# A first stage in groups of 4, 4, 4, 2 and 2 row tiles, and a sequence stage with its weight slabs in pairs between the products

## The chip, the cores and the metric

One core of one Trainium2 chip runs the whole layer as one program. The time is the device time of a launch in microseconds (us). The core has a tensor engine (PE), a vector engine (DVE), an activation engine (ACT), GpSimd (POOL) and a sync engine (SP) that issues most DMAs; 16 DMA engines move the data.

## The reference

The reference is one layer of a generative backbone: 256 latent tokens `x` and 256 context tokens `ctx`, 2048 wide, float32. What matters here:

- `adaln`: `silu(c) @ ada_w + ada_b` gives six rows of 2048 (shift, scale and gate for two halves of the layer). For the context only the first two (shift and scale) are needed, with `c_ctx`. `ada_w` is 2048 x 12288, 100 MB.
- `hx = modulate(rmsnorm(x), sh1, sc1)`, and the same for the context. The input projection `hx @ w_in` follows; its columns from `COL_XBC` on feed the state-space branch (a short convolution, then SiLU), 64 columns feed its step sizes `dt`.
- `ssd_chunked`: a state-space scan in chunks of 128 tokens, 32 heads in 4 groups, forward and backward. Per group: the product of the `C` and `B` rows (`cb`), the states of the chunks, decay matrices `exp(cumulative sums)` per head, the product of `cb * decay` with the inputs inside a chunk (diagonal part) and of `C` with the carried state.
- then a gated norm, a second branch (Hyena, long convolutions whose filters come from a small sine network), output projections and a mixture of experts. The change doesn't touch these.

## The kernel before

Weights stream through a ring of 8 slots (`k.raw`, `RAW = 8`), each slot one slab of 128 partitions x 1024 float32, 512 KB. SP issues the loads in a fixed order, and before a load it waits until the old content of that slot was used; so one late user stops all later loads. A weight for a projection is split into a high and a low half (`w_hi` by ACT, `w_lo` by DVE, each a ring of 4) and multiplied three times (`mm3`): high with high, high with low, low with high. The slabs of `ada_w` are used as they are: PE multiplies them with 32 columns (`cpad`) into strips of 32 partitions of one bank, four strips side by side.

First stage (the block that follows line 325). It needs shift and scale for 16 row tiles of 128 rows. The kernel works in 8 groups of 2 row tiles. A group's ring order is 1 projection slab (two row tiles of `w_in`, 512 columns) and 8 modulation slabs (each 4 row tiles of `ada_w` by 256 columns: four for the shift, four for the scale). PE does for a group `ada(g)` (the 8 slabs, bank 4 or 6 in turn), DVE copies the bank to `mrow` (`mod_rows`, line 526), PE turns the rows into columns (`columns`, line 399), DVE adds bias and gain (`mod_columns`, lines 573 and 576). Then ACT writes the high half of the modulated tokens (line 503), DVE the full value and the low half (lines 585 and 592), and `project` (lines 193 to 195, with the `dt` products at 425 and 426) adds this group's part to four banks. PE's order is `ada(g)`, `columns(g - 1)`, `project(g - 2)`. Ahead of it stand `ada(0)`, `ada(1)` and the transposes of the normed tokens (`tokens`, line 408). Between, DVE reduces the argument of the filter network's sine twice (`sine_argument`, lines 530 to 540); `columns(0)` and `columns(3)` wait for it, since it reads the bank that they write. SP issues the first 8 slabs, then 13 small loads of vector rows, then the rest of the slabs.

Sequence stage (the block that follows line 967). A loop of 4 passes, one for each group of 8 heads. Each pass also consumes 32 slabs of `ada_w` (row tile `j // 2`, half `j % 2` of 2048 columns, so rows of 4 KB) into bank 0 for one of the four other modulation rows. PE's order in a pass is: `cb` (line 1006), 8 slabs, the states (lines 1014 to 1017, banks 1 to 4), 8 slabs, the carried products (line 1023, banks 5, 6, 7, 1), the decay blocks `between(0)` and `between(1)` (lines 1034 and 1035, banks 2 and 3), 4 slabs, `within(0)` (line 1044, banks 4 and 5), `between(2)`, 4 slabs, `within(1)`, `between(3)`, 4 slabs, `within(2)`, 4 slabs, `within(3)`. ACT takes the exponential of a decay block (line 1084), DVE mixes it with `cb` (`mixing`, line 1162) for `within`. DVE computes `hin` from the states (lines 1144 to 1151) before the carried products can start, and reads these (lines 1176 to 1182) between `mixing(1)` and `mixing(2)`. `cb` of the next pass waits for ACT's copies of `B` and `C` (lines 1066 and 1067), which wait until DVE has finished `y` of this one (line 1188). At the end of a pass ACT copies bank 0 out (line 1097), POOL adds the bias and stores the row; the block ends only when the last store has landed.

```python
for n in range(RAW, PER_GROUP * GROUPS1 + RAW):
    g, r = (n - RAW) // PER_GROUP, (n - RAW) % PER_GROUP
    if r == 0:
        sp.wait_ge(st.lo_ready, g + 1)
    else:
        sp.wait_ge(s.raw_used, 8 * g + r)
```

## Time and profile before

| | us |
|---|---|
| median of 3 runs | 2368.26 (2367.81 to 2368.78) |
| the profiled execution | 2367.48 |
| its span on the core | 2365.9 |

| engine | busy us | share of the span |
|---|---|---|
| PE | 2195.0 | 93% |
| DVE | 1529.5 | 65% |
| ACT | 1042.3 | 44% |
| POOL | 105.3 | 4% |

The mean granted clock of PE over the span is 0.968 of full speed. The page gives busy shares by slice and the costliest groups; the timeline gives the instructions of one engine in order of time (start in us, duration of the merged entry, engine, line, operation, output from input, number of records, and in brackets the idle time before it and what ended it). A float32 product of PE appears as two records. The view by stretch gives one line for each stretch: the stretch and its length, then for PE, PE's weight loads, DVE, ACT and POOL the busy us and (in brackets) the instructions, then the granted clock (1.00 is 2.4 GHz), the busy share of the DMA engines (it can come out a little over 1) and GB/s.

### The profile page before, as it was taken

Reading aid. Unit: us, or ns where it says so; the run is one execution under the profiler, and the core shown is the slowest. Engines: PE = TensorE matmul, PEld = TensorE weight load, DVE = VectorE, ACT = ScalarE, POOL = GpSimd, SP = SyncE. Lnnn points to the kernel's source line nnn. Section 1 sums busy time; section 2 is a strip of 40 time slices with the busy share of each in tenths; the row PEclk is TensorE's granted clock in tenths of the full one; section 3 lists DMA queues with packets and bytes.
Section 4 is the critical chain, followed back from the end, with each engine's and each line's share of the span. In section 5 each row is a group of like instructions: output and inputs, shape, how many; then the busy total and the mean of one; then the engine's idle time right before and its main releaser. Section 6 shows DMA issues by size and latency. Waiting matters only on the chain. (4 is left out here: it accounts for less than half of the span.)

```text
span 2365.9 us, 32045 instructions
## 1 busy us (share of the span) xinstructions
PE 2195.0 (93%) x12178; PEld 1770.5 (75%) x12178; DVE 1529.5 (65%) x2085; ACT 1042.3 (44%) x1347; POOL 105.3 (4%) x120
## 2 busy tenths in 40 slices
PE   4899998998899999999999999996899999999995
PEld 1568886444689977777778999985688888778784
DVE  2346565566464577877775454554677777899897
ACT  3324332121464433333333334443655555677774
POOL 1000000000000012120201100000000000000000
PEclk9889999999999999999999999997999999999997
DMA  9872324989657654443433565752388888899993
GB/s 308 268 245 91 98 82 150 342 325 355 193 179 232 181 143 137 124 145 116 129 112 107 150 186 167 234 178 92 118 271 265 293 277 264 310 360 386 352 361 135
DMA packets 322075, 500.64 MB, mean 212 GB/s; under 512 B 16710, under 2 KB 185249, under 8 KB 320535
## 3 DMA queue, kind: packets, MB, share of 16 engines
q1 hardware_dynamic: 317158, 481.02, 61.8%
q0 software_dynamic: 4784, 17.83, 2.2%
q8 instruction: 86, 1.41, 0.3%
q14 instruction: 47, 0.38, 0.0%
HBM read 496.65 MB, written 2.13 MB: 211 GB/s over the span
## 5 line engine op out<-in xcount | busy, mean ns | idle before, releaser
L187 DVE TENSOR_TENSOR w_lo<-raw,w_hi 128x1024 fp32r<-128x1024 f32 x712 | 865.5, 1237 | 474.9 <-ACT w_hi L183 457.2
L183 ACT ACTIVATE w_hi<-raw 128x1024 fp32r<-128x1024 f32 x712 | 743.0, 1058 | 684.9 <-PE bank L195 512.2
L193 PE MATMUL bank<-h,w_hi 128*128 128x256 f32 (+1 forms) x896 | 297.8, 332 | 6.9 <-DVE w_lo L187 4.3
L194 PE MATMUL bank<-h,w_hi 128*128 128x256 f32 (+1 forms) x896 | 293.3, 327 | 0.0
L195 PE MATMUL bank<-h,w_lo 128*128 128x256 f32 (+1 forms) x896 | 293.1, 327 | 0.0
L1419 PE MATMUL bank<-h,w_hi 128*128 128x512 f32 x768 | 275.1, 402 | 0.0
L1421 PE MATMUL bank<-h,w_lo 128*128 128x256 f32 x768 | 215.6, 281 | 0.0
L193 PEld LDWEIGHTS bank<-h,w_hi 128*128 128x128 f32 x896 | 174.9, 195 | 21.6 <-DVE w_lo L187 4.5
L194 PEld LDWEIGHTS bank<-h,w_hi 128*128 128x128 f32 x896 | 175.0, 195 | 13.3 <-issue 0.5
L195 PEld LDWEIGHTS bank<-h,w_lo 128*128 128x128 f32 x896 | 174.4, 195 | 13.8
L1419 PEld LDWEIGHTS bank<-h,w_hi 128*128 128x128 f32 x768 | 144.9, 189 | 37.7 <-issue 3.7
L1421 PEld LDWEIGHTS bank<-h,w_lo 128*128 128x128 f32 x768 | 145.6, 190 | 1.4 <-issue 1.4
L193 PE MATMUL bank<-ys_hi,w_hi 128*128 128x256 f32 x512 | 145.0, 283 | 0.0
L195 PE MATMUL bank<-ys_hi,w_lo 128*128 128x256 f32 x512 | 144.9, 283 | 0.0
L194 PE MATMUL bank<-ys_lo,w_hi 128*128 128x256 f32 x512 | 144.9, 283 | 0.0
L193 PE MATMUL bank<-w_hi,ys_hi 128*128 128x512 f32 x256 | 103.3, 404 | 18.4 <-DVE w_lo L187 18.3
L193 PE MATMUL bank<-w_hi,h 128*128 128x512 f32 x256 | 101.6, 397 | 9.5 <-DVE w_lo L187 9.5
L193 PE MATMUL bank<-w_hi,hidt_hi 128*128 128x512 f32 x256 | 101.7, 397 | 4.3 <-DVE hidt_lo L2662 2.6
L193 PE MATMUL bank<-w_hi,mt_hi 128*128 128x512 f32 x256 | 101.2, 395 | 4.6 <-DVE w_lo L187 4.6
L195 PE MATMUL bank<-w_hi,ys_lo 128*128 128x512 f32 x256 | 101.0, 395 | 0.0
L194 PE MATMUL bank<-w_lo,ys_hi 128*128 128x512 f32 x256 | 100.9, 394 | 0.0
L194 PE MATMUL bank<-w_lo,h 128*128 128x512 f32 x256 | 100.4, 392 | 0.0
(430 smaller groups left out, 3612.5 us busy)
## 6 DMA issues: line engine op xcount, KB each, us to landing
raw<-in_w_in SPq DMA_DIRECT2D x240, 512.0 KB, 4.2
raw<-in_ada_w SPq DMA_DIRECT2D x192, 512.0 KB, 7.1
raw<-in_moe_w_gate SPq DMA_DIRECT2D x128, 512.0 KB, 5.2
raw<-in_moe_w_up SPq DMA_DIRECT2D x128, 512.0 KB, 5.9
raw<-in_moe_w_down SPq DMA_DIRECT2D x128, 512.0 KB, 6.3
raw<-in_w_ssd_out SPq DMA_DIRECT2D x32, 512.0 KB, 4.7
raw<-in_w_hy_out SPq DMA_DIRECT2D x32, 512.0 KB, 3.4
raw<-in_w_o SPq DMA_DIRECT2D x32, 512.0 KB, 4.6
```

The lines of the kernel that those rows point to most:

```text
L183: act.activation(self.k.w_hi[:, j % HL, :], self.k.raw[:, j % RAW, :], ACT.Copy).then_inc(self.hi_ready, 1)
L187: dve.tensor_tensor(self.k.w_lo[:, j % HL, :], self.k.raw[:, j % RAW, :], self.k.w_hi[:, j % HL, :].bitcast(F32), ALU.subtract).then_inc(s ...
L193: pe.matmul(out, lhs[0], rhs[0], start=start, stop=False)
L194: pe.matmul(out, lhs[0], rhs[1], start=False, stop=False)
L195: return pe.matmul(out, lhs[1], rhs[0], start=False, stop=stop)
L1419: mm = pe.matmul(bank[:], st.hi(j, 4)[:, kk, cols], h_both[:, :, 0, kt, :], start=(kt == 0), stop=False)
L1421: mm = pe.matmul(bank[:, 0:L], st.lo(j, 4)[:, kk, cols], k.h_hi[:, 0, kt, :], start=False, stop=(kt == KT - 1))
```

## The change

First stage: the 16 row tiles are worked in 5 groups of 4, 4, 4, 2 and 2. A modulation slab of a group of 4 holds 2 row tiles of `ada_w` by 512 columns, one of a group of 2 still 4 by 256. Shift and scale have a bank each (4 and 6) and are copied to `mrow` separately, each as soon as its half is complete. The ring order becomes a list: the 16 slabs of group 0, then for each further group two projection slabs and its 16 (or 8) modulation slabs. PE's order is written out: single slabs stand between the transposes and between the projections, which go by single row tile. ACT and DVE split the projection slabs in pairs, and the first two during the transposes.

Sequence stage: `ada` takes its slabs in pairs by first and end. The first 4 slabs of a pass stand ahead of the wait for the staged `B` and `C`; the decay blocks 0 and 1 stand directly after the states; the carried products follow as a function of their own (`carried`), and fewer slabs at a time stand between the products. The banks change: carried products 1 to 4, decay blocks 6 and 7, diagonal blocks 5 and 1. The number of products, copies and bytes is the same in both stages, but for `mrow`'s copies (10 for 8).

```diff
-        PER_GROUP, GROUPS1, AHEAD = 9, KT // 2, 3
+        AHEAD = 3
...
+        TILES1 = (4, 4, 4, 2, 2)
+        FIRST1 = (0, 4, 8, 12, 14)
+        LAST1 = len(TILES1) - 1
+
+        def slabs_of(g):
+
+            return 4 * TILES1[g]
+
+        MOD, PROJ = "mod", "proj"
+        order1 = [(MOD, 0, j) for j in range(slabs_of(0))]
+        for g in range(1, LAST1 + 1):
+            for m in range(2 * g - 2, 2 * g):
+                order1.append((PROJ, m, 0))
+            order1 += [(MOD, g, j) for j in range(slabs_of(g))]
+        place1 = {slab: n for n, slab in enumerate(order1)}
...
+            kind, g, j = order1[n]
+            if kind == PROJ:
                 return w_in[:, 2 * g:2 * g + 2, COL_XBC:COL_XBC + 512]
-            half, q = (r - 1) // 4, (r - 1) % 4
-            return ada_w[:, 4 * q:4 * q + 4, half * D + g * 256:half * D + (g + 1) * 256]
+            width, rows_ = TILES1[g] * P, SUB // (TILES1[g] * P)
+            half, q = j // (KT // rows_), j % (KT // rows_)
+            at = half * D + FIRST1[g] * P
+            return ada_w[:, rows_ * q:rows_ * (q + 1), at:at + width]
...
-                for n in range(RAW, PER_GROUP * GROUPS1 + RAW):
-                    g, r = (n - RAW) // PER_GROUP, (n - RAW) % PER_GROUP
-                    if r == 0:
+                for n in range(RAW, len(order1) + RAW):
+                    kind, g, j = order1[n - RAW]
+                    if kind == PROJ:
                         sp.wait_ge(st.lo_ready, g + 1)
                     else:
-                        sp.wait_ge(s.raw_used, 8 * g + r)
-                    st.load(sp, n, first_src(n) if n < PER_GROUP * GROUPS1 else xbc_src(1, n - PER_GROUP * GROUPS1))
+                        sp.wait_ge(s.raw_used, mods_done(g, j))
+                    st.load(sp, n, first_src(n) if n < len(order1) else xbc_src(1, n - len(order1)))
...
+                def mods(g, first, end):
+
+                    for j in range(first, end):
+                        n = place1[MOD, g, j]
+                        width, rows_ = TILES1[g] * P, SUB // (TILES1[g] * P)
+                        half, q = j // (KT // rows_), j % (KT // rows_)
+                        if g and q == 0:
+                            pe.wait_ge(s.mrow, 2 * g - 1 + half)
                         pe.wait_ge(st.full[n % RAW], 16 * (n // RAW + 1))
-                        for m in range(4):
-                            mm = pe.matmul(bank[32 * m:32 * m + 32, half * 256:(half + 1) * 256], k.cpad[:, 4 * q + m, :],
-                                           st.slot(n, 4)[:, m, :], start=(q == 0), stop=(q == 3))
+                        for m in range(rows_):
+                            kt = rows_ * q + m
+                            mm = pe.matmul(k.psum[4 + 2 * half][32 * (kt % 4):32 * (kt % 4) + 32, 0:width], k.cpad[:, kt, :],
+                                           st.slot(n, rows_)[:, m, :], start=(kt < 4), stop=(kt >= KT - 4))
                         mm.then_inc(s.raw_used, 1)
...
-                ada(1)
+                mods(0, 12, 16)
+                mods(1, 0, 1)
                 pe.wait_ge(s.norm, 4)
-                for kt in range(KT):
-                    tokens(kt)
+                for j in range(8):
+                    tokens(2 * j)
+                    tokens(2 * j + 1)
+                    mods(1, j + 1, j + 2)
                 columns(0)
+                mods(1, 9, 13)
                 pe.wait_ge(s.xt, KT)
                 pe.wait_ge(s.cols, 4)
                 pe.wait_ge(s.dt_lo, 1)
-                for g in range(2, GROUPS1):
-                    ada(g)
-                    columns(g - 1)
-                    project(g - 2)
-                    if g == 3:
-                        pe.wait_ge(s.hm, 1)
-                        pe.wait_ge(s.mod, 5)
-                        for half in range(2):
-                            rows_ = slice(half * FILT, (half + 1) * FILT)
-                            mm = pe.matmul(k.psum[7][rows_, 256:512], fw2[rows_, :], k.hmid[rows_, :], start=True, stop=True)
-                        mm.then_inc(s.h1mm, 1)
-                columns(GROUPS1 - 1)
-                project(GROUPS1 - 2)
-                project(GROUPS1 - 1)
+                project(0)
+                mods(1, 13, 16)
+                project(1)
+                mods(2, 0, 1)
+                columns(1)
+                project(2)
+                mods(2, 1, 3)
+                project(3)
+                for kt in range(4, 8):
+                    mods(2, 3 * kt - 9, 3 * kt - 6)
+                    project(kt)
+                pe.wait_ge(s.hm, 1)
+                pe.wait_ge(s.mod, 3)
...
+                mm.then_inc(s.h1mm, 1)
+                mods(2, 15, 16)
+                mods(3, 0, 3)
+                columns(2)
+                mods(3, 3, 5)
+                project(8)
+                mods(3, 5, 7)
+                project(9)
+                mods(3, 7, 8)
+                project(10)
+                mods(4, 0, 2)
+                columns(3)
+                project(11)
+                mods(4, 2, 6)
+                project(12)
+                mods(4, 6, 8)
+                project(13)
+                columns(4)
+                project(14)
+                project(15)
...
+                    if kt in (1, 3):
+                        slab_high(kt // 2)
+
+                act.wait_ge(s.xt, KT)
+                for g in range(LAST1 + 1):
+                    if 0 < g < LAST1:
+                        slab_high(2 * g)
+                        slab_high(2 * g + 1)
+                    if g in (0, 3):
+                        act.wait_ge(s.h1arg, 2 if g else 1)
                         act.activation(k.hmid[:], farg[:, 0, :], ACT.Sin).then_inc(s.hm, 1)
-                    act.wait_ge(s.mod, 2 * g + 2)
-                    for kt in (2 * g, 2 * g + 1):
-                        for v in range(2):
-                            ins = act.activation(k.h_hi[:, v, kt, :], xt[:, v, kt, :], ACT.Identity,
-                                                 bias=k.modc[:, 0, kt, v:v + 1], scale=k.modc[:, 1, kt, v:v + 1])
-                        ins.then_inc(s.hi, 1)
+                    highs(g)
...
-                mod_rows(0)
-                slab_low(1)
                 dve.wait_ge(s.h1mm, 1)
                 sine_argument(k.psum[7][:, 256:512], 0, 1)
-                mod_rows(1)
+                mod_rows(0)
+                slab_low(0)
+                slab_low(1)
...
-                for g in range(GROUPS1):
-                    if g == 3:
+                for g in range(LAST1 + 1):
+                    if g == 2:
                         dve.wait_ge(s.h1mm, 2)
                         sine_argument(k.psum[7][:, 256:512], 2, 3)
-                    if g and g + 1 < GROUPS1:
-                        slab_low(g + 1)
+                    if 0 < g < LAST1:
+                        slab_low(2 * g)
+                        slab_low(2 * g + 1)
+                    mod_columns(g)
+                    modulated(FIRST1[g])
+                    for kt in range(FIRST1[g], FIRST1[g] + TILES1[g]):
+                        if kt + 1 < FIRST1[g] + TILES1[g]:
+                            modulated(kt + 1)
+                        lows(kt)
+                    if g < LAST1:
                         mod_rows(g + 1)
-                    mod_columns(g)
-                    for kt in (2 * g, 2 * g + 1):
-                        modulated(kt)
-                    for kt in (2 * g, 2 * g + 1):
-                        lows(kt)
...
+                    def ada(first, end):
+
+                        if first == 0:
                             pe.wait_ge(s.ada_row, g + 1)
-                        for j in range(4 * part, 4 * part + 4):
+                        for j in range(2 * first, 2 * end):
                             st.wait_full(pe, g, 32, j)
                             ada_strips(pe, k.psum[0], j, st.slot(j, 1)).then_inc(s.ada_used, 1)
 
+                    ada(0, 2)
                     pe.wait_ge(s.staged, g * 2 + 2)
...
                     mm.then_inc(s.cb, 1)
-                    ada(0)
-                    ada(1)
+                    ada(2, 4)
                     pe.wait_ge(s.xw, g + 1)
                     for d in range(2):
                         for t in range(TT):
...
-                    ada(2)
-                    ada(3)
-                    pe.wait_ge(s.hin, g + 1)
-                    for bank, c, state in ((5, 0, h0[:, 0, :]), (6, 0, hin[:, 1, :]), (7, 1, hin[:, 0, :]),
-                                           (1, 1, h0[:, 1, :])):
-                        mm = pe.matmul(k.psum[bank][:], cgt[:, c * P:(c + 1) * P], state, start=True, stop=True)
-                    mm.then_inc(s.yoff, 1)
-
                     def between(z):
...
-                            o = k.psum[2 + z % 2][:, h * P:(h + 1) * P]
+                            o = k.psum[6 + z % 2][:, h * P:(h + 1) * P]
...
-                                mm = pe.matmul(k.psum[4 + c][:, hh:hh + HDIM], mix[:, z % 2, d, h, :],
+                                mm = pe.matmul(k.psum[5 - 4 * c][:, hh:hh + HDIM], mix[:, z % 2, d, h, :],
...
+                    def carried():
+
+                        pe.wait_ge(s.hin, g + 1)
+                        for bank, c, state in ((1, 0, h0[:, 0, :]), (2, 0, hin[:, 1, :]), (3, 1, hin[:, 0, :]),
+                                               (4, 1, h0[:, 1, :])):
+                            mm = pe.matmul(k.psum[bank][:], cgt[:, c * P:(c + 1) * P], state, start=True, stop=True)
+                        mm.then_inc(s.yoff, 1)
+
                     between(0)
+                    ada(4, 5)
                     between(1)
-                    ada(4)
+                    ada(5, 6)
+                    carried()
+                    ada(6, 8)
                     within(0)
                     between(2)
-                    ada(5)
+                    ada(8, 10)
                     within(1)
+                    ada(10, 11)
                     between(3)
-                    ada(6)
+                    ada(11, 13)
                     within(2)
-                    ada(7)
+                    ada(13, 16)
                     within(3)
...
-                    for c, fwd, bwd in ((0, 5, 6), (1, 7, 1)):
+                    for c, fwd, bwd in ((0, 1, 2), (1, 3, 4)):
...
-                        own.inc(dve.tensor_tensor(y, y, k.psum[4 + c][:], ALU.add))
+                        own.inc(dve.tensor_tensor(y, y, k.psum[5 - 4 * c][:], ALU.add))
```

## Rows read from the trace of the kernel before

**Rows 1.** Busy time of each engine by stretch, first stage after the transposes' start

```profile
62.00:170.00 108.00, 93.85 (x673) 66.96 (x672) 41.77 (x86) 28.11 (x46) 0.00 (x0) 0.87 0.83 264
...
62.00:70.00 8.00, 3.71 (x61) 2.11 (x60) 4.33 (x9) 5.55 (x9) 0.00 (x0) 1.00 0.03 8
```

**Rows 2.** SyncE's queue in order of time: start, duration of issue, what

```profile
27.78 1.31 SPq L339 DMA_DIRECT2D p_rows<-in_norm_g  x1
...
69.28 0.51 SPq L155 DMA_DIRECT2D raw<-in_w_in  x1
```

**Rows 3.** Timeline of PE, first stage: start, us, line, tiles

```profile
52.77 8.93 PE L408 MATMUL bank<-tri,p_toks 128*128 128x128 f32 x64
...
75.56 0.77 PE L193 MATMUL bank<-h,w_hi 128*128 128x512 f32 x1
```

**Rows 4.** Timeline of PE, first stage, at the full clock

```profile
84.27 3.66 PE L387 MATMUL bank<-raw,cpad 128*32 128x256 f32 x64
...
87.86 1.05 PE L399 MATMUL bank<-small,p_mrow 128*128 128x2 f32 x8
...
163.34 0.39 PE L193 MATMUL bank<-h,w_hi 128*128 128x512 f32 x1
...
169.46 0.39 PE L426 MATMUL bank<-h,p_wdt_s 128*128 128x512 f32 x1
```

**Rows 5.** Timeline of DVE, first stage: sine argument, chain to the lows

```profile
96.02 0.54 DVE L530 TENSOR_SCALAR p_farg<-bank,p_fvec 128x256 f32<-128x256 f32 x1 [3.79 <-PE bank L458]
...
98.94 1.23 DVE L521 TENSOR_TENSOR w_lo<-raw,w_hi 128x1024 fp32r<-128x1024 f32 x1
...
157.02 0.17 DVE L573 TENSOR_TENSOR modc<-bank,vcol 128x8 f32<-128x8 f32 x1 [4.00 <-PE bank L399]
...
158.72 0.68 DVE L592 TENSOR_TENSOR h<-p_full,h 128x512 fp32r<-128x512 f32 x1
```

**Rows 6.** Stretches with a full DMA queue: 1 KB, 4 KB, 2 KB rows

```profile
42.00:44.00 2.00, 1.35 (x12) 0.41 (x16) 2.00 (x4) 0.00 (x0) 0.00 (x0) 1.00 1.10 349
...
460.00:466.00 6.00, 5.22 (x29) 0.74 (x23) 2.89 (x5) 0.00 (x0) 0.00 (x0) 1.00 1.02 412
...
2072.00:2074.00 2.00, 1.30 (x6) 0.81 (x5) 2.00 (x3) 1.74 (x2) 0.00 (x0) 1.00 1.05 387
```

**Rows 7.** The same view, first and last pass of the sequence stage

```profile
394.00:444.00 50.00, 45.52 (x280) 23.44 (x280) 28.10 (x77) 9.65 (x24) 2.17 (x3) 0.90 0.83 307
...
545.00:592.00 47.00, 43.26 (x280) 22.94 (x280) 28.10 (x78) 9.36 (x24) 2.05 (x3) 0.96 0.95 351
```

**Rows 8.** Timeline of PE, the second pass, and the last pass's end

```profile
447.07 1.22 PE L1006 MATMUL bank<-p_cgt,p_bgt 128*128 128x128 f32 x4 [2.96 <-ACT p_cgt L1067]
...
453.75 3.70 PE L1014 MATMUL bank<-p_xw,p_bg 128*128 128x512 f32 x8
...
459.10 3.11 PE L264 MATMUL bank<-raw,cpad 128*32 128x512 f32 x20
...
465.95 1.13 PE L1023 MATMUL bank<-p_h,p_cgt 128*128 128x512 f32 x2
...
469.49 0.38 PE L1034 MATMUL bank<-tri,p_spans 128*128 128x128 f32 x2
...
473.15 1.92 PE L264 MATMUL bank<-raw,cpad 128*32 128x512 f32 x16
...
475.01 2.00 PE L1044 MATMUL bank<-p_xsg,p_mix 128*128 128x64 f32 x16
...
476.84 0.44 PE L1034 MATMUL bank<-tri,p_spans 128*128 128x128 f32 x2
...
487.68 2.00 PE L1044 MATMUL bank<-p_xsg,p_mix 128*128 128x64 f32 x16 [1.36 <-DVE p_mix L1162]
...
489.61 3.54 PE L264 MATMUL bank<-raw,cpad 128*32 128x512 f32 x16
...
589.92 2.00 PE L1044 MATMUL bank<-p_xsg,p_mix 128*128 128x64 f32 x16
```

102 lines of the change are left out of this document (51 added, 51 removed).

## The prediction

> **What bounds the kernel now.** I read the page first: the tensor engine (PE) is busy in 93% of the span, so most of the program leaves nothing to hide work behind. The stretches where that fails are what the change touches. The table of engine times by stretch, the second view, shows the first one: from 62 to 170 us PE is busy 93.9 of 108 us at a mean granted clock of 0.87. The clock has two levels, 1.2 and 2.4 GHz, so that is 2 x 0.13 x 108 = 28 us at the lower level, some 14 us lost, and 14 us idle. Inside it, from 62 to 70 us, the DMA engines are idle (share 0.03) [rows 1]. The DMA queue's own view says why: the load into the slot of projection slab 2 leaves only at 69.28, because it waits until that slab is split, and the split stands behind the modulation of group 0; all later loads queue behind it [rows 2]. PE pays with idle time, and its first projection starts at 75.56 [rows 3]. The stage's last product starts at 169.46 [rows 4].
>
> The second place is the sequence stage. There the four passes take 51 us down to 47 us each; in the first PE is busy 45.5 of 50 us and the DMA engines 0.83 of the time at 307 GB/s, in the last 43.3 of 47 us and 0.95 at 351 GB/s [rows 7]. Neither is full: the PE timeline of one pass has 2.96 us idle at the turn, 1.36 us before the third product, and stretches at the lower clock, where 16 records take 3.54 us that take 1.92 us otherwise [rows 8].
>
> **Supply.** A slab is 524,288 bytes. Three stretches in which the queue never ran dry show its price by length of contiguous row: 1 KB rows 349 GB/s, 2 KB rows 387, 4 KB rows 412 [rows 6], that is 1.50, 1.35 and 1.27 us a slab. Of the first stage's 64 modulation slabs, 48 go from 1 KB rows (256 columns) to 2 KB rows (512 columns); 16 stay. The saving in supply is 48 x 0.15 = 7 us. The Trainium skill (DMA: Bandwidth & Descriptors, Specifications) puts the least transfer for line rate at 512 B; by that, 1 KB and 2 KB rows would cost the same and these 7 us would be nothing. The trace disagrees: 349 against 387 GB/s.
>
> **First stage, up to the transposes.** Today the transposes start at 52.77, when 16 modulation slabs are consumed [rows 3]. In the new order they start after 17 modulation and 2 projection slabs. The first 8 slabs are issued before the vector rows, and their 1 KB descriptors clog the queue until 27.8 us; only then the rows go out, and no slab is issued meanwhile [rows 2]. With half as many descriptors all of this is out early. I put slab 7 at 30 us (9.3 MB with the tokens and tables at 349 GB/s [rows 6] is 27; 3 more for the start and the short rows), slab 15 eight slabs of 1.35 later, at 41, and three more (two for the projection) at 45. So the transposes start at T = 45, 7.8 us earlier. Bounds: 40 and 51 us.
>
> **First stage, after T.** What PE then does is the same work in another order. Prices at the full clock: 8 modulation slabs 3.66 us (0.46 each), a group of four column products 1.05, and a projection of two row tiles 28 matmuls at 0.227 = 6.4 us (163.34 to 169.46 plus one) [rows 4]. In the new order the transposes alternate with slabs 19 to 26 of the load order. The loads into the slots of the two projection slabs now wait for splits that run in the transposes' shadow (ACT after the copies of tiles 1 and 3, DVE after each), about T+4 and T+7; supply has a hole of some 3 us instead of 8. Slab 26 is consumed at T+12, the columns take until T+13.5, and the chain from columns to the first lows takes 2.4 us (157.02 to 158.72 plus 0.68) [rows 5]; the first projection starts at T+16.5 = 61.5 instead of 75.56. Left for PE: 8 x 6.4 = 51.2, 35 slabs x 0.46 = 16.1, columns 24 x 0.26 = 6.2, the filter product 0.6: 74 us. On top come three waits that the order still has:
> - columns(2) waits for the second sine argument, which DVE starts only after the filter product and mod_rows(2): 2.9 us of DVE (96.02 to 98.94) [rows 5] against four slabs (1.9 us) on PE: 2.3 us;
> - project(8) waits for the modulation of group 2, which DVE reaches after two splits (2 x 1.23): 1.9 us;
> - project(14) follows columns(4) directly, so the whole 2.4 us chain is bare; before, a projection stood in between.
>
> That is 6.6 us, and the stage ends at T+16.5+74+6.6 = T+97. The lower clock: PE fell to it in this stage after waits of 3 to 7 us. I expect it at the first projection (PE is loosely filled before) and after the two places of waits, three times some 6 us at half speed, 8.5 us lost instead of 14. End: 45+97+8.5 = 150.5, against 169.9. Gain 19. Bounds: 8 (T at 51, the clock losses as before) and 29 (T at 42, no clock loss). Supply isn't the limit after T: the last slab of the stage needs its slot from projection slab 7, split at about T+73, and lands by T+79, before its use at T+83. The second stage is one chain of PE products whose head waits for nothing from here but the last projection, so the gain is kept.
>
> **Sequence stage, PE's work in a pass.** From one pass of the timeline [rows 8]: four slabs 1.86 us (473.15 to 475.01), so 32 slabs 14.9; states 5.35 (453.75 to 459.10); carried products 3.54 (465.95 to 469.49); four decay blocks 4 x 1.83 (two in 469.49 to 473.15) = 7.3; four diagonal blocks 4 x 1.83 (475.01 to 476.84) = 7.3; the first product 0.6 at the full clock. Sum 39.0. The supply's floor is 32 x 1.27 = 40.7.
>
> **What goes.** The turn: 2.96 us idle, in which PE now consumes four slabs (1.86), leaving 1.1; but the states then come 5.5 us after the last diagonal block and xw on DVE is ready only 6.1 after it, 0.6 more idle. The 1.36 us: mixing(0) waited for a decay block that stood behind 8 slabs and the carried products; now the decay blocks stand directly behind the states in banks 6 and 7, DVE reaches mixing(2) 17 us after the states and PE needs it 23 us after. And the DMA holes: rate fell whenever PE was 6 to 7 us away from the slabs. Now the longest absence is states plus one decay block, 7.2 us, once a pass, against 8 slots that hold 10 us of supply. So a pass is 39.0 + 1.7 = 40.7 by PE, 40.7 by supply; two limits that meet give a little more than either, and I add 2.3 for slab waits and a clock dip. 43 us.
>
> Pass 0 begins at about 394.4, when stage 2 ends. PE now eats four slabs before the first product, mostly at the low clock, so the states end at about the same time (407), and 30.4 us later (24 slabs 11.2, 7.3, 7.3, 3.5, 1 for waits) the pass ends at 437.5. Three more at 43 give 566.5. Before, the last diagonal block ended at 589.92 + 2.00 = 591.9 [rows 8]. Gain 25. Bounds: 36 (no waits beyond 40.7 and 435 for pass 0) and 11 (below). The tail, from the last slab through ACT, POOL and a store that the block waits for, stays.
>
> **Sum.** 2367.5 (this execution) - 19 - 25 = 2323.5; the runs' median is 0.8 higher and inside any error here. I say 2323.
>
> **Rivals.**
> A. Supply stays as it is. In the fastest pass the DMA engines were busy 0.95 at 351 GB/s [rows 7]; if the missing rate isn't from holes but from packets that run slower beside PE, ACT and DVE traffic, a pass can't go below 16.8 MB / 351 = 47.8 us. The sequence stage then gains 6.6 + 3 x 1.5 = 11: 2337. For it: busy share near 1 with rates far apart; against: 412 GB/s for 6 us while PE worked [rows 6]. The Trainium skill (DMA: Bandwidth & Descriptors, Specifications) gives about 358 GB/s as the HBM limit per core, which would mean the same, 46.9 us a pass; the trace has 412.
> B. The first stage gains only 8, by its bounds above: 2334. For it: three chains that stand bare.
> C. The clock holds at 2.4 GHz in both stages since the long waits are gone: 29 + 36 would be the whole, 2302; with some of it 2308.
> D. Slower. The clock: in the sequence stage PE now waits a little after nearly every product, and each wait could put it at 1.2 GHz. At share h of a pass's work in the low level a pass is 40.7 + 39h. It decides from h = 0.34: there a pass takes 54.1, four of them 216.5 against 197.5 now, which eats the other gain of 19 too. With h = 0.5 it is 60.2 a pass, 43 more than now, less 19: 2392. For it: the 1.36 us wait is followed by 3.5 us at half speed (489.61) [rows 8]; against it: six microseconds with a wait before each pair kept clock 1.00 [rows 6]. The Trainium skill (TensorE: Matmul & The Clock Gate, "A second HAM failure mode") tells of such oscillation from many small idles; the trace shows it after the longer ones only.
>
> **Numbers.** Forecast 0.60, A 0.12, B 0.12, C 0.11, D 0.04, and 0.01 that nothing moves. Its own range is 2314 to 2332; with A, B and most of C, 2306 to 2342. Faster by over 0.2% (4.7 us, about what this kernel's runs can tell from no change) 0.95, within it 0.01, slower 0.04.
>
> **What would show it.** Transposes near 45 us and no DMA hole of 8 us after them; first projection near 61; the stage's end near 150. In the sequence stage DMA share near 1.0 at 390 GB/s or more, passes of 43 us, no idle before within(2), the turn's idle near 1 us. Passes of 47 with a full share mean A; a mean clock under 0.8 there means D. I would be wrong at the root if the stage after either one took back the time.

## The result, and the profile after

The changed kernel takes 2351.22 us (median of 4 runs, 2350.11 to 2351.67) against 2368.52 of the kernel before in the same runs: ratio 0.9932, interval 0.9920 to 0.9943. It is faster by 17.3 us, where some 45 were forecast, and outside the range of 2306 to 2342. The profiled execution (the one whose trace is read below) took 2350.11 us, its span 2348.5 at a mean granted clock of 0.975 (before: 2367.48, 2365.9, 0.968). One execution of the changed kernel in a later series (`e12`) took 3686.06 us at a granted clock of 0.555, and is left out of its ratio.

The gain is split by two marks on ACT, the table load with which the sequence stage begins and the first high half of the block behind it (before: 394.35 and 599.07). Timeline of ACT after (start, duration, engine, line, operation, records, idle time before and its releaser):

```profile
390.80 1.28 ACT L1132 ACT_TABLE_LOAD   x1 [0.57 <-DVEq L1168]
...
582.97 3.90 ACT L183 ACTIVATE w_hi<-raw 128x1024 fp32r<-128x1024 f32 x4 [8.32 <-PEq L1029]
```

The sequence stage starts 3.5 us earlier and ends 16.1 us earlier: 3.5 come from the first stage (forecast 19), 12.6 from the sequence stage (forecast 25), 1.2 from the rest. That is one trace against one trace: in the traces of all these kernels the second stage, which no edit touches, takes 221.7 to 226.6 us from the first stage's last product to the first mark (224.9 before, 224.7 here, 221.7 in `e12`), and the changed sequence stage between the marks takes 192.2 here and 193.9 in `e12`, for 204.7. PE's timeline of the first stage after, against [rows 3, 4]:

```profile
33.81 1.05 PE L409 MATMUL bank<-raw,cpad 128*32 128x512 f32 x4 [0.34 <-DMA raw<-in_ada_w]
...
45.92 1.05 PE L409 MATMUL bank<-raw,cpad 128*32 128x512 f32 x4 [0.31 <-DMA raw<-in_ada_w]
50.07 1.92 PE L409 MATMUL bank<-raw,cpad 128*32 128x512 f32 x4 [3.10 <-DMA raw<-in_ada_w]
51.93 1.97 PE L432 MATMUL bank<-tri,p_toks 128*128 128x128 f32 x8
...
56.83 1.05 PE L409 MATMUL bank<-raw,cpad 128*32 128x512 f32 x4
57.81 1.09 PE L432 MATMUL bank<-tri,p_toks 128*128 128x128 f32 x8
...
71.72 1.92 PE L409 MATMUL bank<-raw,cpad 128*32 128x512 f32 x16
...
74.43 0.47 PE L193 MATMUL bank<-h,w_hi 128*128 128x512 f32 x1 [0.79 <-DVE h L651]
...
89.21 1.06 PE L409 MATMUL bank<-raw,cpad 128*32 128x512 f32 x8
...
98.89 1.91 PE L409 MATMUL bank<-raw,cpad 128*32 128x512 f32 x12
...
119.99 2.78 PE L423 MATMUL bank<-small,p_mrow 128*128 128x2 f32 x16 [2.33 <-DVEq L600]
122.70 1.94 PE L409 MATMUL bank<-raw,cpad 128*32 128x256 f32 x16
125.35 0.76 PE L193 MATMUL bank<-h,w_hi 128*128 128x512 f32 x1 [0.71 <-DVE h L651]
...
158.21 0.62 PE L193 MATMUL bank<-h,w_hi 128*128 128x512 f32 x1 [2.56 <-DVE h L651]
...
166.06 0.39 PE L450 MATMUL bank<-h,p_wdt_s 128*128 128x512 f32 x1
```

The transposes begin at 51.93, the first projection stands at 74.43 and the last product at 166.06 (169.46 before). A slab of two row tiles by 512 columns is x4 here. Read its price by what stands alone: one slab between two transposes takes 57.81 - 56.83 = 0.98 us, a pair 1.06, three 1.91, four 1.92 (these three are durations of entries; from start to start they are 1.00, 1.84 and 1.86). An odd slab costs as much as two.

The DMA queue of SP after (start of the issue, duration of the entry), against [rows 2]:

```profile
2.38 15.14 SPq L155 DMA_DIRECT2D raw<-in_ada_w  x8
17.57 4.71 SPq L360 DMA_DIRECT2D p_rows<-in_norm_g  x1
...
27.50 0.42 SPq L360 DMA_DIRECT2D p_rows<-in_ada_b  x1
27.97 7.34 SPq L155 DMA_DIRECT2D raw<-in_ada_w  x8
```

The same place in the queue before the change:

```profile
33.01 0.42 SPq L339 DMA_DIRECT2D p_rows<-in_ada_b  x1
33.48 0.42 SPq L155 DMA_DIRECT2D raw<-in_ada_w  x1
```

The eight first slabs have half as many descriptors, and the first vector row now leaves SP at 17.57 instead of 27.78 [rows 2], the last at 27.50 instead of 33.01, slab 8 at 27.97 instead of 33.48. So the queue did come free 5.5 us sooner, but the transposes start only 0.8 us sooner.

The stretches after (columns as in [rows 1]), against [rows 1, 7]:

```profile
16.00:24.00 8.00, 2.79 (x8) 0.38 (x8) 0.00 (x0) 4.62 (x5) 0.00 (x0) 1.00 0.76 249
54.00:62.00 8.00, 8.00 (x42) 3.32 (x41) 2.45 (x2) 5.66 (x9) 0.00 (x0) 0.88 0.43 111
51.93:166.45 114.52, 108.12 (x610) 67.94 (x608) 41.88 (x84) 38.04 (x62) 0.00 (x0) 0.92 0.79 262
400.00:570.00 170.00, 165.17 (x1049) 85.15 (x1047) 107.71 (x291) 33.67 (x84) 7.33 (x9) 1.00 0.94 356
434.00:444.00 10.00, 9.32 (x54) 3.40 (x52) 6.74 (x17) 4.94 (x12) 2.49 (x3) 1.00 1.03 411
446.00:462.00 16.00, 16.00 (x88) 8.13 (x86) 11.40 (x33) 3.52 (x10) 0.00 (x0) 1.00 0.77 276
452.00:454.00 2.00, 2.00 (x17) 1.16 (x18) 1.92 (x4) 1.76 (x5) 0.00 (x0) 1.00 0.07 29
```

The third line runs from the transposes to the end of the stage. The same stretch before (52.77 to 169.90):

```profile
52.77:169.90 117.13, 103.08 (x744) 76.15 (x740) 42.46 (x87) 35.44 (x60) 0.00 (x0) 0.88 0.85 270
```

These two lines hold the answer for the first stage. Idle is length less busy time: 14.0 before, 6.4 after. What the clock took is (1 - clock) times the length: 14.1 and 9.2. What is left is PE's work at the full clock: 89.0 and 99.0. So 7.6 us of idle time and 4.9 us of clock went, and 9.9 us of work came: 2.6 us net, and 0.8 from the earlier start. The clock is shown in hundredths, so each of these is good to about 0.6 us. This reckoning has a flaw: a low clock costs nothing while PE is idle, and some 2 us of the 14.1 fell into waits, most of them from 70 to 72.8 us. Taken microsecond by microsecond, with the clock weighted by PE's busy time, the clock took 11.8 and 8.4 us and the work is 91.3 and 99.7. So 3.4 us of clock went and 8.4 us of work came; the answer stays, with a smaller number. In the sequence stage the clock is 0.52 for the first 3.2 us (390.8 to 394) and 1.00 from there on. At the end of pass 0 the DMA engines are full at 411 GB/s and PE waits for slabs; 12 us later they are nearly idle. PE's timeline from the end of pass 0, against [rows 8]:

```profile
439.65 0.71 PE L1069 MATMUL bank<-p_cgt,p_bgt 128*128 128x128 f32 x4
440.30 1.99 PE L264 MATMUL bank<-raw,cpad 128*32 128x512 f32 x8
442.51 1.05 PE L264 MATMUL bank<-raw,cpad 128*32 128x512 f32 x4 [0.23 <-DMA raw<-in_ada_w]
...
444.78 3.70 PE L1076 MATMUL bank<-p_xw,p_bg 128*128 128x512 f32 x8
...
451.91 1.06 PE L264 MATMUL bank<-raw,cpad 128*32 128x512 f32 x8
...
480.67 2.00 PE L1098 MATMUL bank<-p_xsg,p_mix 128*128 128x64 f32 x16
...
485.83 0.71 PE L1069 MATMUL bank<-p_cgt,p_bgt 128*128 128x128 f32 x4
```

`cb` opens at 439.65 and 485.83, then at 532.39: passes of 46.2 and 46.6 us, where 43 were forecast. The turn has no idle of 2.96 us any more and the third product no wait. What remains is one line of the waits of PE's weight loads from 400 to 575 us (engine, line, waited for; us in all, times, longest). These are waits of the weight loads; PE's own idle time from 400 to 570 us is 4.8:

```profile
PEld bank L264 <- DMA raw<-in_ada_w: 30.4, 32, 1.8
```

### The profile page after: what moved, and what is told of

Same layout as the page of the kernel before. It is cut to its first block and busy times, and to the rows that moved or that the text cites. A ratio compares the mean times of both kernels' runs of the same rounds, so it can differ in the third digit from the quotient of the medians.

```text
span 2348.5 us, 31655 instructions
## 1 busy us (share of the span) xinstructions
PE 2202.4 (94%) x11986; PEld 1757.5 (75%) x11986; DVE 1527.5 (65%) x2081; ACT 1043.3 (44%) x1347; POOL 105.4 (4%) x120
## 5 line engine op out<-in xcount | busy, mean ns | idle before, releaser
L193 PE MATMUL bank<-w_hi,mt_hi 128*128 128x512 f32 x256 | 101.3, 396 | 5.1 <-DVE w_lo L187 5.0
L195 PE MATMUL bank<-w_hi,hidt_lo 128*128 128x512 f32 x256 | 100.2, 391 | 0.0
```

Of the source, the lines that this page charges most:

```text
L193: pe.matmul(out, lhs[0], rhs[0], start=start, stop=False)
L195: return pe.matmul(out, lhs[1], rhs[0], start=False, stop=stop)
```

## The experiments

A ratio is to the kernel before in runs on the same chip. A difference between ratios of two chips is good to some 5 or 6 us (add the intervals), and the changed kernel itself has two: 0.9932 and, in `e12`, 0.9916, which are 4 us apart. Gains "by the ratios" below are against the first; against the second they are 4 us less. "T" is the start of the transposes. The profiled executions of one first stage differ by 1.5 to 3 us (T 50.4 to 51.9, last product 163.1 to 166.1), mostly by the clock; so the first stage is compared by the three terms from T to its last product, taken from one line of each trace as above. The last column is the work with the clock weighted by busy time:

| kernel | length | idle | lost to the clock | work | work, weighted |
|---|---|---|---|---|---|
| before | 117.1 | 14.0 | 14.1 | 89.0 | 91.3 |
| changed | 114.5 | 6.4 | 9.2 | 99.0 | 99.7 |
| changed, again (`e12`) | 111.9 | 7.3 | 5.6 | 99.0 | 100.0 |
| slabs in pairs (`e4`) | 107.2 | 8.2 | 5.4 | 93.6 | 94.5 |
| narrow slabs (`e5`) | 111.6 | 6.7 | 10.0 | 94.8 | 95.8 |
| chains ahead (`e8`) | 102.7 | 2.4 | 1.0 | 99.3 | 99.8 |
| all three (`e9`) | 101.3 | 2.9 | 5.1 | 93.3 | 94.2 |

**One stage each.** The two edits on their own. `e1` has the new first stage with the old sequence stage, `e2` the other way round.

> The first stage changed, the sequence stage as before. If the two parts don't touch each other, the first stage alone gives what its own end shows in the changed kernel: its end came 3.4 us sooner, so 2365 us, and the sequence stage's passes keep 51, 49 and 48 us. If the gain there leans on the sequence stage, or is given back in the second stage, the time is 2368.

> The first stage as before, the sequence stage changed. By its own span in the changed kernel (12.7 us shorter) and the 1 us that came behind it: 2355 us, passes of 45.5 to 46.6 us. If the sequence stage gained only because it started with a fuller ring, less: 2360.

Measured: `e1` 2361.68, ratio 0.9987 (0.9978 to 0.9997), 3.4 us off; `e2` 2350.85, ratio 0.9942 (0.9926 to 0.9959), 14.3 us off. Together 17.7 against 17.3 of the whole: within the intervals (some 2 and 4 us) nothing was lost between the parts, and each falls short by itself. The traces are less tidy: in `e1`'s the unchanged sequence stage takes 202.2 us for 204.7, and its first mark is 2.3 us earlier. The marks on ACT in `e2`:

```profile
393.33 1.28 ACT L1070 ACT_TABLE_LOAD   x1 [0.57 <-DVEq L1106]
...
585.92 3.90 ACT L183 ACTIVATE w_hi<-raw 128x1024 fp32r<-128x1024 f32 x4 [8.18 <-PEq L967]
```

192.6 us between them, 192.2 in the changed kernel, 204.7 before.

**Half the bytes in the sequence stage.** Is a pass long by PE's work or by the supply?

```diff
-                st.feed(sp, GROUPS, 32, lambda i, j: ada_src(i + 2, j), s.ada_used, lambda j: z_src(0, j))
+                def half_src(i, j):
+                    return ada_w[:, j // 2:j // 2 + 1, ds((i + 2) * D + (j % 2) * SUB, SUB // 2)]
+
+                st.feed(sp, GROUPS, 32, half_src, s.ada_used, lambda j: z_src(0, j))
```

> In the sequence stage each slab of the modulation weights loads only its first 512 of 1024 columns (the other half of a slot keeps what was in it, so four of the modulation rows are not computed); PE's work is unchanged. Theory 1 (rhythm: PE spends the middle of a pass away from the slabs, the ring fills and the DMA engines stop, and PE then waits for slabs at the end): without the scarcity a pass falls from 46 to 41 us, the sum of PE's work and the two waits at the turn, and the kernel to 2332. Rival (PE's own work in a pass is longer than my 39.0 because products and slabs alternate): it stays at 44 or more. If it falls to 41, the forecast's price of PE's work in a pass was right.

The kernel leaves out half of each slab, so it doesn't compute four of the modulation rows; its products in PE are the same. Measured: 2331.01 in one run. PE in `e3`:

```profile
435.51 0.71 PE L1075 MATMUL bank<-p_cgt,p_bgt 128*128 128x128 f32 x4 [1.11 <-ACT p_cgt L1139]
...
477.24 0.71 PE L1075 MATMUL bank<-p_cgt,p_bgt 128*128 128x128 f32 x4 [0.70 <-ACT p_cgt L1139]
```

From one `cb` to the next pass 0 takes 41.1 us (394.37 to 435.51) and the two behind it 41.7. The prediction's 40.7 for PE alone, its idle turn included, was right to 1 us. The 4.4 to 5.0 us that a later pass of the changed kernel takes beyond 41.7 are supply.

**The same slabs at an even pace.** In the changed kernel two, four or six slabs stand between products, and none inside the states and the carried products. Here two stand in every gap, those inside included, and the last six ahead of the last diagonal block (`ada` counts pairs).

```diff
-                    ada(2, 4)
+                    ada(2, 3)
                     pe.wait_ge(s.xw, g + 1)
...
+                    ada(3, 4)
                     pe.matmul(k.psum[3][:], bg[:, 0, :], xw[:, 4, :], start=True, stop=True)
...
+                    ada(4, 5)
                     between(0)
-                    ada(4, 5)
+                    ada(5, 6)
                     between(1)
-                    ada(5, 6)
+                    ada(6, 7)
                     carried()
...
+                            if bank == 3:
+                                ada(7, 8)
```

> The changed kernel with the sequence stage's slabs at an even pace: a pair also in the middle of the states, behind them, and in the middle of the carried products, and two slabs less in the middle of the turn, so PE is never more than 3.5 us from the slabs. Theory 1 (rhythm, the ring goes dry in the middle): the DMA engines don't stop, a pass comes to 42 to 43 us, the kernel 12 us faster than the changed one, 2339. Rival A of the prediction (supply is slower beside PE's traffic): the passes stay at 46, 2351.

Measured: 2341.29, ratio 0.9899 (0.9882 to 0.9915), by the ratios 7.8 us below the changed kernel; the stage takes 184.3 us (389.16 to 573.50) for 192.2. The stretches of `e7`:

```profile
400.00:570.00 170.00, 163.43 (x1080) 84.95 (x1076) 108.70 (x292) 34.26 (x85) 9.09 (x11) 1.00 1.01 376
446.00:462.00 16.00, 16.00 (x106) 7.90 (x105) 12.90 (x35) 3.52 (x10) 0.00 (x0) 1.00 1.01 389
```

The 16 us that had 276 GB/s have 389, the waits for slabs fall from 30.4 to 9.5 us, and the passes take 44.2, 44.0 and 44.5 us from one last diagonal block to the next, for 46.1, 46.6 and 46.7. So filling the hole gave back 2.2 to 2.6 us a pass. The hole alone would be worth more: (411 - 276) GB/s over 16 us are 2.2 MB, 5.3 us at 411. The rest wasn't won because 44 is above the expected floor: with a share of 1.01 all through, the rate is 376 and not 411 GB/s, and 32 slabs at 376 take 44.6 us. The 376 is a mean of two levels, which return in each pass of `e7`:

```profile
438.00:456.00 18.00, 17.75 (x96) 7.45 (x92) 13.05 (x44) 4.13 (x13) 0.56 (x1) 1.00 1.02 406
458.00:480.00 22.00, 21.39 (x175) 13.06 (x176) 13.49 (x31) 3.38 (x5) 1.84 (x2) 1.00 1.00 355
```

In the next pass it is 410 and 359. The DMA engines are as busy in the second half and move an eighth less. That is what rival A expected, in half of a pass; what slows the packets there no run shows.

**Slabs in pairs in the first stage.** Tests the price of an odd slab.

```diff
-                for j in range(8):
-                    tokens(2 * j)
-                    tokens(2 * j + 1)
-                    mods(1, j + 1, j + 2)
+                for j in range(4):
+                    for kt in range(4 * j, 4 * j + 4):
+                        tokens(kt)
+                    mods(1, 2 * j + 2, 2 * j + 4)
...
+                project(4)
+                mods(2, 8, 10)
+                project(5)
+                mods(2, 10, 14)
```

> The changed kernel, but the first stage's slabs of two row tiles are taken in even numbers everywhere (between every four transposes a pair, between the projections 2 or 4). Theory 2 (a slab of 2 row tiles by 512 columns uses two of the four strips, so one alone costs PE 0.98 us and not 0.46; 16 places with an odd number of them cost 0.5 us each): 8 us less PE work between the transposes and the filter product, less 1 for a pair that is waited for, 7 us faster than the changed kernel: 2344 on its scale of 2351. Rival (the stage is late because slabs arrive late, not because PE works longer): 2351 or slower, since a pair is waited for.

Measured: 2344.71, ratio 0.9892 (0.9869 to 0.9914). PE in `e4`:

```profile
55.83 1.97 PE L432 MATMUL bank<-tri,p_toks 128*128 128x128 f32 x16
57.73 1.06 PE L409 MATMUL bank<-raw,cpad 128*32 128x512 f32 x8
58.73 1.53 PE L432 MATMUL bank<-tri,p_toks 128*128 128x128 f32 x12
```

Two slabs stand where one did and take the same 1.0 us. The work falls by 5.2 to 5.4 us, the clock's loss by 3.8 against the changed kernel's first profile and by nothing against its second. One slab has moved ahead of T (606 records for 610), which is 0.5 to 1 us of the 5.3. So the price of the odd slabs is shown, at 4 to 5 us; the total of 9.5 us by the ratios (5.7 against `e12`'s) holds some clock as well.

**Narrow slabs.** All modulation slabs four row tiles by 256 columns, as before the change, in the new order.

```diff
-                        for m in range(rows_):
-                            kt = rows_ * q + m
-                            mm = pe.matmul(k.psum[4 + 2 * half][32 * (kt % 4):32 * (kt % 4) + 32, 0:width], k.cpad[:, kt, :],
+                        for m in range(4):
+                            mm = pe.matmul(k.psum[4 + 2 * half][32 * m:32 * m + 32, 256 * part:256 * part + 256],
+                                           k.cpad[:, 4 * q + m, :], st.slot(n, 4)[:, m, :], start=(q == 0), stop=(q == 3))
```

> The changed kernel, but groups of 4 row tiles also load slabs of 4 row tiles by 256 columns (1 KB rows, four strips in each slab), in the same order. Theory 2: PE gains 8 us in the odd places, supply loses 0.15 us on each of the 16 slabs ahead of the transposes (2.4), the rest of the supply is covered: 5 us faster than the changed kernel, 2346. If supply by row length decides the stage, as my 7 us had it: 7 us slower, 2358.

Measured: 2352.03, ratio 0.9924 (0.9901 to 0.9948), between the changed kernel's two. The profiled execution is its fastest (2344.90). PE in `e5`:

```profile
54.58 1.97 PE L429 MATMUL bank<-tri,p_toks 128*128 128x128 f32 x8
...
60.65 0.64 PE L406 MATMUL bank<-raw,cpad 128*32 128x256 f32 x8
61.22 1.09 PE L429 MATMUL bank<-tri,p_toks 128*128 128x128 f32 x8
```

Here both expectations are half right and cancel. A lone slab that fills four strips takes 61.22 - 60.65 = 0.57 us instead of 0.98, and the work falls by some 4 us. But loads of 1 KB rows come slower: T is 54.58, 2.7 later.

**The start.** The vector rows go out on POOL's queue after the first slabs, so that slab 8 doesn't wait behind them (`e6`); the `dt` weights, whose loads run beside the first slabs, go out later (`e10`).

```diff
+                for name, n in VEC_ROWS[2:]:
+                    k.vector_rows(pool, name, n)
```

```diff
+                pool.wait_ge(s.raw_used, 14)
                 pool.dma_start(wdt[:], w_in[:, :, COL_DT:COL_HY]).then_inc(s.wdt, 16)
```

> The changed kernel with the 13 loads of vector rows issued by POOL instead of SP. In the changed kernel SP issued them from 17.6 to 28.0 us and slab 8 only then, though its slot was free at 15.7. If this blocking made the transposes late (51.9 for a forecast of 45): slab 8 goes out at 18, the transposes start 4 us sooner, 2347. If the DMA engines were full anyway (busy share 0.9 to 1.06 from 22 to 50 us) and only their 4 us at half rate from 18 to 22 count: 1 us, 2350.

> The changed kernel with the load of the step weights (2048 runs of 256 B, issued by POOL at 9 us) held back until 14 modulation slabs are used, and its split behind the transposes' first half. The DMA engines moved 183 to 306 GB/s from 16 to 24 us with that load in their queues. If its short runs make this dip: the first slabs land 2 to 3 us sooner, the transposes start at 48.5, the kernel is 3 us faster than the changed one. If the dip is the end of the token loads and the slots that SP left empty: no change, transposes at 51.

Measured: `e6` 2350.97, ratio 0.9920 (0.9894 to 0.9945), T 51.05; `e10` 2349.55, ratio 0.9922 (0.9891 to 0.9952), T 49.58. `e6`'s T lies within the 50.4 to 51.9 of the unchanged start: with no vector row ahead of slab 8, PE gets its slabs no sooner, so SP's queue wasn't what held T. In `e10` slab after slab was there earlier, yet the stage's last product stands at 163.76, which the changed kernel reaches as well (163.05 in `e12`). Neither moves the time by an amount that these runs can tell. The stretch of 16 to 24 us in `e10`:

```profile
16.00:24.00 8.00, 3.36 (x8) 0.38 (x8) 0.00 (x0) 4.54 (x5) 0.00 (x0) 1.00 0.78 270
```

Without the `dt` weights the dip is no smaller than in the changed kernel (249, and 277 in `e12`). What makes it stays open.

**The chains ahead.** DVE takes the second sine argument and the splits of the next two slabs before `mod_rows(2)`, the filter product stands after `project(5)`, and `columns(4)` before `project(13)`, which covers the last chain.

```diff
-                mods(4, 2, 6)
-                project(12)
-                mods(4, 6, 8)
-                project(13)
-                columns(4)
-                project(14)
+                mods(4, 2, 8)
+                project(12)
+                columns(4)
+                project(13)
+                project(14)
```

> The changed kernel with three chains moved off PE's path: the filter product after projection 5 and the sine argument and the splits of slabs 4 and 5 ahead of mod_rows(2); columns(4) ahead of projection 13, all of group 4's slabs before it. The three waits (2.3, 0.7 and 2.6 us in the changed kernel) go. If the fall of the clock after them (1.2 GHz from 120 to 131 and at 158 to 162, 7 us lost) hangs on these waits too, 11 us faster: 2340. If the clock falls anyway: 5, 2346.

Measured: 2342.79, ratio 0.9873 (0.9848 to 0.9899). The line of `e8` from T to its last product:

```profile
51.63:154.35 102.72, 100.35 (x610) 63.70 (x608) 42.14 (x84) 38.12 (x62) 0.00 (x0) 0.99 0.87 293
```

The three waits were 2.33, 0.71 and 2.56 us; 1.58 remains, before `project(8)`. Idle falls by 4.0 us and the clock's loss by 8.2, against `e12` by 4.9 and 4.6; the work stays. So the clock behind the three waits cost at least about as much as the waits. The edit moves all three chains at once, so what each of them was worth isn't shown.

**All together, and the changed kernel again.** `e9` is pairs, chains and even pace; `e11` adds the start's two edits; `e12` is the changed kernel beside them on the same chip.

> Slabs in pairs, the chains ahead, and the even pace in the sequence stage together. If the three causes are separate, their gains add: 7 and 11 in the first stage, 10 in the sequence stage, 28 less than the changed kernel: 2323, which is where the prediction had the change itself. If pairs and chains share their gain (the same lower clock counted twice), 2328.

> As the last, with the vector rows on POOL and the step weights late: 1 us for the rows and 3 for the step weights on top, 2319; if the start is bound by bytes alone, the same as the last.

> The changed kernel itself, beside the three others on one chip, since the kernel before came out between 2365 and 2371 on two chips: 2351 if the chip's level is that of the first result; its ratio to before stays 0.993. The transposes' start tells how far one execution of the same order lies from another (so far 50.4 to 51.9 us).

Measured: `e9` 2331.93, ratio 0.9839 (0.9815 to 0.9862); `e11` 2331.57, ratio 0.9842 (0.9807 to 0.9877); `e12` 2347.86, ratio 0.9916 (0.9890 to 0.9942). Both beat the kernel before by 1.6% and the changed one by 0.8%, but three edits that gave 9.5, 14 and 7.8 us by the ratios give 22 together. Against `e12`'s ratio they are 5.7, 10.2 and 4.0, and together 18.2: by that measure hardly anything is missing, so the times don't settle whether the gains add. What happened in the first stage the trace shows. The stretches of `e9`:

```profile
52.83:154.10 101.27, 98.34 (x606) 64.99 (x604) 42.27 (x84) 37.65 (x62) 0.00 (x0) 0.95 0.86 294
62.00:92.00 30.00, 28.65 (x164) 17.09 (x164) 14.50 (x32) 14.50 (x26) 0.00 (x0) 1.00 1.05 386
62.00:118.00 56.00, 53.07 (x325) 31.89 (x322) 23.72 (x53) 19.18 (x34) 0.00 (x0) 0.99 1.00 355
118.00:122.00 4.00, 4.00 (x11) 3.03 (x11) 3.75 (x7) 3.56 (x7) 0.00 (x0) 0.50 1.09 362
```

The last product is at 153.71, no earlier than with the chains alone (153.96). The table says where the pairs' gain went: the work is down by 6.0 against `e8` (5.6 by the weighted column), as it should be, and the clock took 4.1 back. The same wait of 1.58 us before `project(8)` that left the clock alone in `e8` is followed by 0.50 here. Beside it the DMA engines' share is now 1.00 from 62 to 118 us, T comes 1.2 us later, and the second stage takes 226.6 us from the last product to the mark, the upper end of its spread of 221.7 to 226.6. The sequence stage takes 184.3 us (380.26 to 564.58) against 192.2. The profiled execution of `e9` is its slowest (2336.87), so what its trace shows behind these stages isn't counted.

## Why the prediction was wrong

The mechanisms were there, and sizes failed in both stages: in the first the start T and the price of PE's slabs, in the second the supply.

**T (forecast 45, range to 51; measured 51.93).** Slab 7 was put at 30 and is consumed at 33.81; slab 15 at 41, now 45.92; from there 6.0 instead of 4 us, 0.9 of it because the slab at 50.07 stands alone behind a 3.10 us wait and runs at the low level. The cadence of 1.35 us a slab was right. The failing step is "With half as many descriptors all of this is out early. I put slab 7 at 30 us". The queue did come free, 10.2 us sooner for the first row and 5.5 for slab 8, but it wasn't the limit (`e6`). Bytes fit better: from 24 to 46 us the DMA engines' share is 1.05, at 340 and later 385 GB/s, and up to 33.81 they moved 10.5 MB at a mean of 310 GB/s, for the 9.3 MB at 349 and 3 us that were forecast; from 16 to 24 us the rate was 249. What makes this dip stays open. 6.9 us, which nearly takes the whole of the stage's first term.

**PE's work from T on (forecast 90; measured 99 to 100).** The forecast's 105.5 us from T to the end, less 6.6 of waits and 8.5 of clock, is 90, near the 89.0 (91.3 weighted) that the same stretch has before. The failing step is "35 slabs x 0.46 = 16.1", and with it the eight slabs among the transposes: it took the price of slabs that stand together and use all four strips [rows 4]. A slab of two row tiles uses two of the four, and standing alone it costs 0.98. Eight stand between transposes and one between projections, 9 x 0.5 = 4.5 us, five threes between projections (1.91 for 1.4) 2.4 us; the projections of single row tiles take 3.4 us (79.63 to 83.07) where 3.2 was used, sixteen times, some 3 us. The sum is some 10, for a gap of 9 to 10 to the forecast. Of it `e4` and `e5` take back 4 to 5 and 4 in two ways that share only the strips; the 3 us of the projections are read from the trace, and no run tests them. It shows first at the first projection, which stands 22.5 us behind T and not 16.5: 4 us for the eight odd slabs and 2 for the low clock of the transposes' first 4 us. The Trainium skill (TensorEngine Tiling (Array Packing), Key Properties) says that tiles of the array work independently of each other; the trace agrees, two slabs take 1.06 and one takes 1.05.

**The waits and the clock (forecast 6.6 and 8.5; measured 6.4 and 9.2, or 8.4 weighted).** Right in size, and the waits nearly to the place: 2.33 us before columns(2) for 2.3, 2.56 before project(14) for 2.4; project(8)'s 0.71 for 1.9 was less, and the first projection waits 0.79. The clock fell in three places as forecast, but the first was the start of the transposes (1.2 GHz from 49 to 56 us) and not the first projection, which ran at 2.4 GHz. That its total came out right is partly luck: `e12`, the same kernel, lost 5.6 us.

**The hole after the transposes (forecast 3 us).** It is 8 us long, at 111 GB/s from 54 to 62 us, but PE was busy all through, so it costs nothing.

**Sequence stage, PE.** Right to 1 us: 40.7 against 41.7 (`e3`); no idle before `within(2)`; the long turn gone.

**Sequence stage, supply (forecast 43 a pass; measured 46.1, 46.6, 46.7 from one last diagonal block to the next, and 45.7 from the mark to the end of pass 0).** Pass 0 was right: it ends at 436.5, forecast 437.5. Two steps failed behind it. The first is "7.2 us, once a pass, against 8 slots that hold 10 us of supply". The states begin at 444.78, and from 452 to 454 the share is 0.07: from 444.78 to 454 the DMA engines moved 2.8 MB, some 5.3 slabs and not eight. My reading, which no run tests, is that a slot frees only when PE has used it, and PE arrived starved, so the loads under way were partly done. And it isn't one absence: between 444.78 and 459.51 PE takes four slabs, where the supply would bring 11. `e7` shows what this costs, 2.2 to 2.6 us a pass. The second step is the floor itself, "32 x 1.27 = 40.7": it took the 412 GB/s of a 6 us stretch for the whole pass, but over whole passes with the share at 1.01 the rate is 376 GB/s (`e7`), which makes 44.6 us. So 43 could not be reached by any order of the slabs that was tried.

**The rivals.** A (no rate above 351) didn't happen: 411 GB/s for 10 us while PE waited for slabs, and 376 over three passes in `e7`. But A holds in weaker form: in the second half of `e7`'s passes a full queue moves 355 and 359 GB/s. The 358 GB/s per core of the Trainium skill, cited in the prediction, doesn't bind. Another page of the Trainium skill (Perfetto Trace Analysis, Engine Utilization) says that a single active core may pass that share, up to about 435, and the trace's 411 agrees with this one. B (first stage gains 8) was too kind: 3.5. C's clock did come in the sequence stage (1.00, where the first pass had 0.90 [rows 7]), but the supply set the pass all the same. D is refuted: clock 1.00 from 400 to 570 us, with 32 waits of PE's weight loads for slabs.

**The range.** The bounds were 8 and 11, the measured gains 3.5 and 12.6. The lower bound of the first stage held only T and the clock open; the price of PE's slabs was taken as known, though the rows of before show no slab of two row tiles by itself in the first stage. The upper bounds were also added up a little wrong: T at 42 and no clock loss end the first stage at 139.1, a gain of 31 and not 29; passes of 40.7 behind a pass 0 that ends at 435 end at 557.1, a gain of 35 and not 36. Neither bears on the outcome.

## What to carry to other kernels

A product that fills only part of the array's strips has a price by its place: count it at what it costs alone wherever something else stands on both sides, and place such products in twos. A ring of slots bridges an absence by what its slots still have to load when the absence starts, so spread the consumers evenly before counting slots. And take the supply's price from a stretch as long as a whole pass, not from its best 6 us. Short waits of PE can cost as much again in clock behind them (three waits of 5.6 us: 4.0 to 4.9 us of idle time and 4.6 to 8.2 of clock came back), but not reliably: the same wait cost it in one kernel and not in another.

## What the runs showed of the hardware

- Two strips busy or four: 1.05 and 1.06 us for one and two slabs of 128x512 float32 products with 32 columns.
- Rates with the DMA engines full, beside PE, ACT and DVE at work, by length of row: 1 KB 350 GB/s (`e5`, 80 to 92 us), 2 KB 386 (`e9`, 62 to 92 us), as in the short stretches of before (349 and 387 [rows 6]). 4 KB rows had 412 there and 406 and 410 in the first halves of `e7`'s passes, but 355 and 359 in the second halves at the same share, 376 over 170 us. What slows them there stays open.
- After waits of 2.3 to 3.1 us PE ran at 1.2 GHz for several us (around the starts at 50.07, 119.99 and 158.21 in the changed kernel). Waits of 0.2 to 0.3 us before slab after slab left it at 2.4 GHz, but in `e5` the level fell already within a wait of 0.87 us (72.28 to 73.15). A wait of 1.58 us did the one in `e9` and the other in `e8`; what decides between them stays open.
- Freed of the vector rows or of the `dt` weights, the loads from 16 to 24 us stay at 245 and 270 GB/s at a share under 0.8 (249 in the changed kernel, 277 in `e12`), against 352 in the next 4 us of the changed kernel. It stays open what holds them.
